# Where the first weight load of a turn stands among the stores of the key/value stage

## The reference, cut to what matters

```python
kv_new = (x @ attn_w_kv).reshape(b, n, N_DIL_GROUPS, 2, HEADS_PER_GROUP, HEAD_DIM)
...
x = layer_norm(ALPHA * x + 0.5 * swiglu(x, ffn_w13[layer, 0], ffn_w2[layer, 0]), ...)
...
q = (x @ w_q).reshape(b, n, N_DIL_GROUPS, HEADS_PER_GROUP, HEAD_DIM) * (HEAD_DIM ** -0.5)
for g, (win, dil) in enumerate(DIL_PATTERNS):          # (128,1), (512,4), (2048,16)
    o, lse = dilated_group_attention(q[:, :, g], k, v, q_offs[g], dil, n_keys, bias)
...
return o.reshape(b, n, ATTN_GROUP_WIDTH) @ w_o
```

## Time and profile before

| what | value |
|---|---|
| median of 3 runs | 2198.03 us (2197.64 to 2198.89) |
| the profiled execution's own time | 2195.15 us |
| its span (first to last instruction) | 2193.5 us |
| PE busy, PEld busy | 2086.8 us (95%), 2014.1 us (92%) |
| DVE busy, ACT busy, POOL busy | 1421.7, 867.4, 228.8 us |
| mean granted TensorE clock | 0.976 of full speed |
| stretch of the key/value turns 2 to 9 | 1432.5 to 1577.7 us from the span's start |

### The profile page before, as it was taken

The page is one execution under the profiler, slowest core; times in us unless marked ns, Lnnn a source line. Parts: engine busy times, 40 slices in busy tenths (PEclk is TensorE's granted clock), DMA queues, the critical chain, the costliest instruction groups (busy, mean ns, idle before and its releaser), DMA issues.

```text
span 2193.5 us, 43507 instructions
## 1 busy us (share of the span) xinstructions
PE 2086.8 (95%) x16575; PEld 2014.1 (92%) x16575; DVE 1421.7 (65%) x2358; ACT 867.4 (40%) x1529; POOL 228.8 (10%) x267
## 2 busy tenths in 40 slices
PE   7999999999999999999999999999978789999998
PEld 7999999999999999999999999998965588999997
DVE  3583895685795597389549835267645377828955
ACT  3341453353453254254325525222234345514533
POOL 0000002304000000410000041111012130000022
PEclk9999999999999999999999999999979799999998
DMA  4242433222233233224423333567586323333331
GB/s 141 72 127 86 126 118 104 77 77 77 72 95 103 72 97 110 73 72 149 122 86 98 100 90 109 204 208 230 166 271 217 112 72 91 102 87 88 99 99 54
DMA packets 381501, 249.80 MB, mean 114 GB/s; under 512 B 10422, under 2 KB 363038, under 8 KB 381326
## 3 DMA queue, kind: packets, MB, share of 16 engines
q1 hardware_dynamic: 371271, 210.00, 32.2%
q0 software_dynamic: 10096, 37.94, 5.0%
HBM read 230.63 MB, written 22.35 MB: 115 GB/s over the span
## 4 chain that ended last, share of the span: by engine, by line
PE 73%; DVE 11%; DMA 6%; issue 4%; ACT 3%; SPq 1%; POOL 1%; DVEq 0%; ACTq 0%; POOLq 0%
PE pair L762 33%; PE pair L894 27%; PE pair L801 5%; DMA t_w_raw<-in_attn_w_kv 3%; PE pair L1022 2%; DMA t_w_raw<-in_ffn_w 2%; DVE t_w_seven L1984 2%; DVE t_w_lo L1862 1%; PE pair L1271 1%; DVE t_w_sum L1979 1%; PE pair L774 1%; DVE t_u_sum L2265 1%; ACT t_w_hi L1400 1%; DVE t_stream L2190 1%; DVE t_u L1988 1%
## 5 line engine op out<-in xcount | busy, mean ns | idle before, releaser
L894 PE MATMUL pair<-t_x_diff_hi,t_w_seven 128*128 128x272 f32 x1960 | 409.9, 289 | 0.0
L1862 DVE TENSOR_TENSOR t_w_lo<-t_w_raw,t_w_hi 128x1024 fp32r<-128x1024 f32 (+2 forms) x152 | 233.0, 1533 | 200.0 <-ACT t_w_hi L1400 194.6
L1400 ACT ACTIVATE t_w_hi<-t_w_raw 128x1024 fp32r<-128x1024 f32 (+2 forms) x152 | 177.3, 1171 | 446.7 <-PE pair L762 374.2
L894 PEld LDWEIGHTS pair<-t_x_diff_hi,t_w_seven 128*128 128x128 f32 x1960 | 320.3, 188 | 0.0
L762 PE MATMUL pair<-t_h_lo,t_w_hi 128*128 128x272 f32 x1232 | 254.8, 288 | 0.0
L762 PE MATMUL pair<-t_h_hi,t_w_lo 128*128 128x272 f32 x1232 | 254.6, 288 | 0.0
L762 PE MATMUL pair<-t_h_hi,t_w_hi 128*128 128x272 f32 x1232 | 254.5, 288 | 0.0
L894 PE MATMUL pair<-t_x_hi,t_w_seven 128*128 128x272 f32 x1120 | 240.7, 295 | 11.2 <-DVE t_c L1988 9.9
L894 PE MATMUL pair<-t_x_diff_lo,t_w_seven 128*128 128x272 f32 x840 | 241.7, 288 | 0.0
L894 PEld LDWEIGHTS pair<-t_x_hi,t_w_seven 128*128 128x128 f32 x1120 | 184.5, 188 | 23.4 <-issue 12.5
L762 PEld LDWEIGHTS pair<-t_h_hi,t_w_lo 128*128 128x128 f32 x1232 | 193.2, 188 | 0.0
(11 more groups left out here) (317 smaller groups left out, 4889.8 us busy)
## 6 DMA issues: line engine op xcount, KB each, us to landing
t_w_raw<-in_ffn_w SPq DMA_DIRECT2D x280, 256.0 KB, 3.0
t_w_raw<-in_ffn_w SPq DMA_DIRECT2D x64, 704.0 KB, 4.7
t_w_raw<-in_ffn_w SPq DMA_DIRECT2D x36, 512.0 KB, 3.7
t_cached<-in_cache_kv_w POOLq DMA_DIRECT2D x16, 1024.0 KB, 8.7
t_cached_v<-in_cache_kv_w POOLq DMA_DIRECT2D x16, 1024.0 KB, 10.6
t_w_raw<-in_attn_w_kv SPq DMA_DIRECT2D x24, 512.0 KB, 7.2
t_w_raw<-in_attn_w_q SPq DMA_DIRECT2D x12, 512.0 KB, 3.9
scratch_bias_rows<-scratch_bias_row SPq DMA_DIRECT2D x12, 384.0 KB
```

Of the source, the lines that this page charges most:

```text
L894: m = nc.tensor.matmul(out[:, 0:HALF], w[:, k, :], b, start=start and k == 0 and j == 0, stop=k == 3 and j == 2, skip_group_check=not start)
L1400: nc.scalar.activation(whi[s][:, 0:KT[stage], :], raw[s][:, 0:KT[stage], :], ACT.Copy) \
L1862: nc.vector.tensor_tensor(wlo[s][:, 0:k, :], raw[s][:, 0:k, :], whi[s][:, 0:k, :].bitcast(F32), ALU.subtract).then_inc(lo_made[s], 1)
```

## The change

W0(i+1) is taken out of its place behind the last store of iteration i and put between the stores, behind the token store of unit 1 (`kv_store(i - 2, 1)`, the second store of an iteration). W1(i+1) stays behind the last store. `stream` gets an argument that says which of the two loads to issue. The two loads of turns 0 and 1 are issued ahead of the loop, as they were in effect before. Each load keeps its own wait. No instruction on PE, DVE, ACT or POOL is moved.

```diff
-            def stream(stage, i):
-                for s in range(2):
+            def stream(stage, i, parts=(0, 1)):
+                for s in parts:
...
-            for i in range(UNITS["kv"]):
-                stream("kv", i)
-                if i >= 1:
-                    kt_store(i - 1, 0)
-                    if i >= 2:
-                        kv_store(i - 2, 1)
-                    kt_store(i - 1, 1)
-                    kv_store(i - 1, 0)
+            stream("kv", 0)
+            stream("kv", 1)
+            for i in range(1, UNITS["kv"]):
+                kt_store(i - 1, 0)
+                if i >= 2:
+                    kv_store(i - 2, 1)
+                if i + 1 < UNITS["kv"]:
+                    stream("kv", i + 1, (0,))
+                kt_store(i - 1, 1)
+                kv_store(i - 1, 0)
+                if i + 1 < UNITS["kv"]:
+                    stream("kv", i + 1, (1,))
```

## The result

| | before | after |
|---|---|---|
| median of the first measurement (4 runs each) | 2197.84 us | 2183.07 us |
| lowest and highest run | 2195.77 to 2198.89 | 2180.14 to 2185.37 |
| ratio, 95% interval | | 0.9936 [0.9922, 0.9951] |
| the profiled execution's span | 2193.5 us | 2178.4 us |
| granted clock, mean | 0.976 | 0.978 |

The kernel became faster, by 14.8 us between the medians, where 9.0 were forecast. The interval of the ratio does not hold 1.

What follows compares the result with a forecast made beforehand. TensorE was taken to bound the stage, delayed by late W0 loads amid cached keys. Span 2193.5 - 9.0 = 2184.5 us, plus 1.65 gives 2186.2, plus 2.9 gives 2189.0; range of 8 in 10: 2186 to 2194.

Steps and rivals of the forecast that it cites:

- Steps 1 to 4: Key/value stage: W0 issued 2.8 us ahead of the turn, lands in 4 to 6 us, worth 9.0 us; W1 costs zero.
- the sum by causes: Turns 3 to 8: TensorE's waits for DVE's product, 7.6 us, plus the half-clock stretch, 1.7 us, together 9.3 us.
- Step 5: Beginning of the stage: earlier W0(2) wins nothing; it could make W1(1) late by at most 1.7 us; taken as 0.
- W1 lands: Rival, turns 3 to 8: W1, with slack of 1.5 us, comes too late; 4.2 us of gain lost, 2193.2 us; chance 0.10.
- the DMA engines: Rival, key/value stage: transfers are the bound, or the token store holds W0 back; nothing changes, 2198 us; chance 0.07.
- the granted clock behind the stage: Rival, attention stage: one full-clock stretch falls to the lower level, costing 17.75 us more, 2206.8 us; chance 0.03.
- step 6: End of the stage: turns 10 and 11 have no such wait; what follows should move forward as a whole.
- the sum: Whole kernel: span 2193.5 - 9.0 = 2184.5 us, execution's own time 2186.2, median of the runs 2189.0.
- the range of 8 us: Whole kernel: measured time expected between 2186 and 2194 us, 8 in 10.
- the last one, the 2.9 us: Whole kernel: the median of the runs lies 2.9 us above the profiled execution, raising 2186.2 to 2189.0 us.

Runs made afterwards that it cites:

- before again: The kernel before, run again with no edit as a control against itself; ratio 0.9999 [0.9986, 1.0012].

## Why the prediction was wrong

**What held.** Steps 1 to 4 held to some tenths of a us: W0 goes 2.85 us ahead of the turn (2.8 forecast), lands in 3.8 us (4 to 6), W1 costs nothing, turns 3 to 8 take 101.8 us (102.2) in three executions of the change. The clock's fall went with the gap, as the sum by causes had assumed. Step 5's zero held, within the scatter of the first turns; that TensorE has no gap there over 0.18 us was one execution's luck, since "before again", in the same order, has 0.66 us. The rivals fell: W1 lands 3.9 us before it is used (1.5 forecast), the DMA engines rise to 0.76 and do not bind, and the granted clock behind the stage stayed as it was (0.93 and 0.94). The rule of the Trainium skill (DMA: Bandwidth & Descriptors, "Issuing engines are not separate DMA queues") agrees with the trace: in 11 us q0 had 63.6% and q1 30.1% of the same engines. But it did not bind here. Moving one load out of the mix was still worth 9.1 to 9.5 us of turns 3 to 8; the engines were not full all turn (0.71 of turn 5).

**The step that failed is step 6**: the sum was set on the median of 3 runs of before, and the range of 8 us was made from the bounds of the change alone. It held no term for how an execution differs from the next with the same instructions. The three runs shown lay within 1.3 us; 17 runs of the same kernel on another occasion went from 2190 to 2202 us, and over 13 profiles the same instructions ahead of the stage took from 1400.6 to 1407.1 us. In terms of the sum, it is the last one, the 2.9 us that lead from the profiled execution (2195.15) up to the median of 3 runs (2198.03). The medians of the kernel before on the three later occasions are 2194.75, 2193.51 and 2196.93, so this term is worth between -1.6 and +1.8 us there. Without it the forecast is 2186.2. The changed kernel measured 2185.63 and 2183.95 on two of these occasions.

In the first measurement both sides lay out of the middle: the kernel before was high (2197.84) and the changed one low (2183.07). How far two medians of 4 can lie apart can be estimated from the later runs. Four drawn at random from the 57 of the kernel before and four from the 12 of the changed one differ in their medians by 6.4 to 14.9 us in 95 of 100 draws. The 14.8 us are at the edge of that.

**How large the change is.** Four measurements contain the order of turns 3 to 8 as changed and nothing else that the traces show to matter: 0.9936, 0.9949, 0.9945 and, from iteration 3 on, 0.9964. Weighted by the inverse squares of their intervals' half-widths (0.00145, 0.00165, 0.0021, 0.0012) they give 0.9951, or 10.8 us, +-0.0008 if they are independent. But the intervals of the lowest and the highest do not meet (up to 0.9951, from 0.9952), so they are too narrow, and so is +-0.0008. By how much the four scatter, +-0.0013 is the fairer estimate: 8 to 14 us. The turns give 9.3 (111.25 and 110.96 against 101.8), which is inside.

**What stays open.** The other parts of the stage and behind it are on the average a little shorter in the new order, but not beyond their scatter. Whether 1 or 2 us more than the 9.3 belong to the change is not settled, nor is why the first measurement read 14.8: scatter can do it, but no run shows that it did.

## What to carry to other kernels

When a load lands late, look not only at its own queue but at what another engine issues at the same time. Here the same 512 KB needed 3.8 us or 11 us by whether 2.36 MB of keys moved with it, and it helped nearly as much to hold the burst back as to issue the load before it. And before a range is written, ask how far executions of the same kernel lie apart; three runs that agree to 1.3 us do not say. The stretch that the change touches tells more: turns 3 to 8 repeat to 0.1 us over three executions of the change, where whole executions differ by 5.

## What the runs showed beside

- In the burst of the changed kernel (1480.6 to 1491.6 us; packets, MB, share of 16 engines) q0 and q1 share the engines as before, although q1 had one weight load less waiting:

```profile
q0 software_dynamic: 624, 2.36, 62.3%
q1 hardware_dynamic: 1593, 1.01, 29.0%
```

- How little a load gets in the burst can be read from the queues' packets. In the kernel with W0 one store later, from 1488.5 to 1493 us, both queues move 362 packets. But a packet of the keys' queue has 3.9 KB on average (1.42 MB / 362), and one of the queue with the weights 0.5 KB. In the kernel before, from 1491 to 1496.5 us, the packets are 442 and 315.

```profile
q0 software_dynamic: 362, 1.42, 85.8%
q1 hardware_dynamic: 362, 0.18, 13.8%
```

- A load that is issued close to a burst is not safe: 0.9 us into the turn, 0.2 us behind POOL's first load, it needed 11.3 us; 2.85 us ahead of the turn, 3.8 us.
- A gap of TensorE of 2.1 us (2.0 in the second execution), behind gaps of 1.5 to 1.9 us in the two turns before, was followed by 3.4 us at 1.2 GHz (granted clock 0.50) in both executions of the kernel before. In the executions that had no gap over 0.4 us in turns 3 to 8, the clock did not fall there.
